# One 512-column product for the high and low halves of the sample's input, in 80 tiles of a two-layer encoder

## The reference

```
D_MODEL, SEQ, DEC_SEQ, DEPTH, D_FF = 1024, 512, 256, 2, 4096

def trunk(x, mem, p):
    for layer in range(DEPTH):
        ...                                     # mixer; its output goes through a 1024x1024 matrix
        x = x + y.astype(x.dtype)
        h = rms_norm(x, p['norm_cross'][layer])
        ...
        x = x + cross_attention(h, m, ...)       # ends in  o.astype(h.dtype) @ w_o
        h = rms_norm(x, p['norm_mlp'][layer])
        x = x + (jnp.square(jax.nn.relu(h @ p['mlp_w1'][layer])) @ p['mlp_w2'][layer]).astype(x.dtype)
    return x
```

## Time and profile before

| | value |
|---|---|
| median of three executions | 2402.44 us |
| the profiled execution's own time | 2402.41 us |
| its span, first to last instruction | 2400.6 us |
| TensorE busy | 2389.2 us (100%) |
| VectorE busy | 1512.3 us (63%) |
| ScalarE busy | 1166.6 us (49%) |
| granted TensorE clock | 1.0 throughout |
| DMA | mean 121 GB/s, weights 512 KB a tile |

### The profile page before, as it was taken

The page is one execution under the profiler, slowest core; times in us unless marked ns, Lnnn a source line. Parts: engine busy times, 40 slices in busy tenths (PEclk is TensorE's granted clock), DMA queues, the critical chain, the costliest instruction groups (busy, mean ns, idle before and its releaser), DMA issues.

```text
span 2400.6 us, 35749 instructions
## 1 busy us (share of the span) xinstructions
PE 2389.2 (100%) x14327; PEld 2050.2 (85%) x14327; DVE 1512.3 (63%) x2554; ACT 1166.6 (49%) x2070; POOL 0.2 (0%) x4
## 2 busy tenths in 40 slices
PE   9999999999999999999999999999999999999999
PEld 6988877888889998998789888888888898888887
DVE  8999668776566555664655438848985565533332
ACT  5334455555445555545454436636764453523432
POOL 0000000000000000000000000000000000000000
PEclk9999999999999999999999999999999999999999
DMA  5446533553124654443234323233234323433332
GB/s 201 106 98 164 209 110 103 165 202 123 62 88 150 192 185 132 132 133 105 76 112 149 96 88 123 89 101 100 89 100 148 122 80 117 126 98 98 97 97 89
DMA packets 109700, 291.36 MB, mean 121 GB/s; under 512 B 18944, under 2 KB 40576, under 8 KB 108256
## 3 DMA queue, kind: packets, MB, share of 16 engines
q1 hardware_dynamic: 100832, 264.83, 35.5%
q10 hardware_dynamic: 8704, 24.25, 3.3%
HBM read 267.45 MB, written 19.50 MB: 120 GB/s over the span
## 4 chain that ended last, share of the span: by engine, by line
PE 86%; DVE 3%; ACT 1%; issue 0%; DVEq 0%; ACTq 0%
PE ps L1499 74%; PE ps L1613 2%; PE ps L1570 2%; PE ps L1595 2%; PE ps L1637 1%; PE ps L1626 1%; DVE wlo L1476 1%; PE ps L1583 0%; DVE ringP L1886 0%; PE ps L1644 0%; PE ps L1991 0%; PE ps L2056 0%; PE ps L1513 0%; DVE in_lP L1893 0%; PE ps L1525 0%
## 5 line engine op out<-in xcount | busy, mean ns | idle before, releaser
L1471 ACT ACTIVATE whi<-wraw 128x1024 fp32r<-128x1024 f32 x430 | 452.1, 1052 | 183.5 <-PE ps L1499 127.1
L1499 PE MATMUL ps<-in_hP,whi 128*128 128x512 f32 x1336 | 532.8, 399 | 1.7 <-DVE in_lP L1893 0.9
L1476 DVE TENSOR_TENSOR wlo<-wraw,whi 128x1024 fp32r<-128x1024 f32 x430 | 522.9, 1218 | 3.1 <-ACT whi L1471 2.9
L1499 PE MATMUL ps<-in_hP,wlo 128*128 128x512 f32 x1336 | 520.8, 390 | 0.0
L1499 PE MATMUL ps<-in_lP,whi 128*128 128x512 f32 x1336 | 520.2, 389 | 0.0
L1499 PE MATMUL ps<-in_hS,whi 128*128 128x256 f32 x1088 | 316.0, 290 | 0.5 <-DVE x L1830 0.5
L1499 PE MATMUL ps<-in_hS,wlo 128*128 128x256 f32 x1088 | 307.7, 283 | 0.0
L1499 PE MATMUL ps<-in_lS,whi 128*128 128x256 f32 x1088 | 307.7, 283 | 0.0
L1499 PEld LDWEIGHTS ps<-in_hP,whi 128*128 128x128 f32 x1336 | 250.8, 188 | 60.5 <-issue 6.6
L1499 PEld LDWEIGHTS ps<-in_hP,wlo 128*128 128x128 f32 x1336 | 250.7, 188 | 53.5
L1499 PEld LDWEIGHTS ps<-in_lP,whi 128*128 128x128 f32 x1336 | 251.0, 188 | 51.7 <-issue 1.4
(11 more groups left out here) (494 smaller groups left out, 3662.6 us busy)
## 6 DMA issues: line engine op xcount, KB each, us to landing
wraw<-wt SPq DMA_DIRECT2D x432, 512.0 KB, 3.5
wraw<-wt ACTq DMA_DIRECT2D x17, 512.0 KB, 4.4
k_scratch<-region_P SPq DMA_DIRECT2D x16, 256.0 KB, 3.1
v_scratch<-vtmp SPq DMA_DIRECT2D x32, 128.0 KB, 3.5
x<-x_in SPq DMA_DIRECT2D x4, 768.0 KB, 7.0
x<-x_in SPq DMA_DIRECT2D x2, 1536.0 KB, 7.1
mix_mem<-mem_in ACTq DMA_DIRECT2D x1, 2048.0 KB, 15.7
region_S<-k_scratch ACTq DMA_DIRECT2D x2, 1024.0 KB, 7.1
```

The costliest lines, as they stand in the source:

```text
L1471: nc.scalar.activation(whi[:, (n + 3) % NHI, :, :], wraw[:, ws(n), :, :], ACT.Copy).then_inc(wh.sem, 1)
L1476: nc.vector.tensor_tensor(wlo[:, ws(n), :, :], wraw[:, ws(n), :, :], whi[:, (n + 3) % NHI, :, :].bitcast(F32), ALU.subtract).then_inc(wr.s ...
L1499: last = nc.tensor.matmul(ps[:, m % 2, 0:N[prod.g]], w_[:, k, :], x_[:, k, :], start=(k == 0 and j == 0), stop=(k == KT - 1 and j == 2))
```

## The change

It concerns tiles of the sample alone, those whose weights are in the list `WIDE`: the output matrix `o0` of the first cross-attention (8 tiles), up00 to up03 and dn00 to dn03 (the whole first MLP, 64 tiles) and `dout`, the output matrix of the second mixer (8 tiles). That is 48 residual tiles and 32 up tiles.

- High and low input parts now lie side by side in one SBUF tensor (`in_S`, `hid_S`; `hid_P` too, whose products are not changed), so that TensorE takes both in one product of 512 columns with the high weights. High x high lands in columns 0 to 255 of the bank, high x low in columns 256 to 511; low x high (256 columns) is accumulated on the first half. A step `k` has two products in place of three.
- Somebody must add the two halves. In residual tiles VectorE adds both to `x`, one after the other, with a semaphore between them. In up tiles VectorE first sums the halves with a `tensor_reduce` from PSUM to `ringS` (which frees the bank), ACT works on `ringS` in SBUF in place of PSUM, and the subtraction for `hid_l` (`dve_up_low`) stands one slot later on VectorE, behind the next low part of weights.

```
@@ trunk_tail
-                hid_h[g] = sb(f"hid_h{g}", [P, KT, N[g]], F32R, on=over)
-                hid_l[g] = sb(f"hid_l{g}", [P, KT, N[g]], F32R, on=over)
+                hid = sb(f"hid_{g}", [P, KT, 2, N[g]], F32R, on=over)
+                hid_h[g], hid_l[g], hid_w[g] = hid[:, :, 0, :], hid[:, :, 1, :], hid[:, :, :, :]
...
-            in_h = {"P": in_hP, "S": sb("in_hS", [P, KT, TS], F32R, on=fl)}
-            in_l = {"P": in_lP, "S": sb("in_lS", [P, KT, TS], F32R, on=fl)}
+            in_S = sb("in_S", [P, 2, KT, TS], F32R, on=fl)
+            in_h = {"P": in_hP, "S": in_S[:, 0, :, :]}
+            in_l = {"P": in_lP, "S": in_S[:, 1, :, :]}
...
+            WIDE = {WT[n] for n in ("dn00", "dn01", "dn02", "dn03", "dout", "o0", "up00", "up01", "up02", "up03", )}
...
@@ pe_tile
+                if prod.g == "S" and prod.wide is not None:
+                    for k in range(KT):
+                        if i == 0 and prod.ready is not None:
+                            pe.wait_ge(*prod.ready(k))
+                        nc.tensor.matmul(ps[:, m % 2, :].rearrange("p (z t) -> p z t", z=2), w_h[:, k, :], prod.wide[:, k, :, :],
+                                         start=(k == 0), stop=False)
+                        last = nc.tensor.matmul(ps[:, m % 2, 0:N["S"]], w_l[:, k, :], h_[:, k, :], start=False, stop=(k == KT - 1))
+                    last.then_inc(td.sem, 1)
+                    return
@@ act_tile
+                elif prod.kind == "up" and prod.wide is not None:
+                    a.wait_ge(tf[b].sem, m // 2 + 1)
+                    both = ring["S"][:, i % 2, :]
+                    act_chain(nc.scalar.activation(both, both, ACT.Relu))
+                    act_chain(nc.scalar.activation(both, both, ACT.Square))
+                    nc.scalar.activation(hid_h[g][:, i, :], both, ACT.Copy).then_inc(z["hx"].sem, 1)
@@ vector engine
+            def dve_up_low(v, t):
+                prod, i, m = t
+                v.wait_ge(gs["S"]["hx"].sem, prod.up.hx + i + 1)
+                nc.vector.tensor_tensor(hid_l["S"][:, i, :], ring["S"][:, i % 2, :], hid_h["S"][:, i, :].bitcast(F32), ALU.subtract)\
+                    .then_inc(low_d.sem, 1)
...
+                    if g == "S" and prod.wide is not None:
+                        dve_chain(nc.vector.tensor_tensor(x[:, i, cols(g)], ps[:, b, TS:2 * TS], x[:, i, cols(g)], ALU.add))
                     nc.vector.tensor_tensor(x[:, i, cols(g)], ps[:, b, 0:N[g]], x[:, i, cols(g)], ALU.add).then_inc(tf[b].sem, 1)
...
+                elif prod.kind == "up" and prod.wide is not None:
+                    v.wait_ge(td.sem, m + 1)
+                    both = ring["S"][:, i % 2, :]
+                    nc.vector.tensor_reduce(both, ps[:, b, :].rearrange("p (z t) -> p t z", z=2), AX.X, ALU.add).then_inc(tf[b].sem, 1)
...
                             lows = t[2] + NHI - 1
+                        if before is not None and before[0].kind == "up" and before[0].wide is not None:
+                            dve_up_low(v, before)
```

More of the change, by code:

```diff
@@ L975, in trunk_tail @@
             fl = ExitStack()
-            hid_h, hid_l, R = {}, {}, {}
+            hid_h, hid_l, hid_w, R = {}, {}, {}, {}
             for g, words in (("P", 12288), ("S", 6144)):
                 over = ExitStack()
-                hid_h[g] = sb(f"hid_h{g}", [P, KT, N[g]], F32R, on=over)
-                hid_l[g] = sb(f"hid_l{g}", [P, KT, N[g]], F32R, on=over)
+                hid = sb(f"hid_{g}", [P, KT, 2, N[g]], F32R, on=over)
+                hid_h[g], hid_l[g], hid_w[g] = hid[:, :, 0, :], hid[:, :, 1, :], hid[:, :, :, :]
                 over.close()
@@ L1048, in trunk_tail @@
             tf = [sig(f"tf{i}") for i in range(2)]
+            low_d = sig("low_d")
             gs = {g: {n: sig(f"{n}_{g}") for n in ("sqd", "sql", "acd", "ssum", "sroot", "snew", "an", "ah", "ar", "ap", "hx",
@@ L1098, in __init__ @@
                     self.hx = gs[g]["hx"].take(KT)
-                    self.m = {}
+                    self.m, self.low = {}, None
                 def ready(self, k):
                     m = self.m[k]
+                    if self.low is not None:
+                        return low_d.sem, self.low + k + 1
                     return tf[m % 2].sem, m // 2 + 1
@@ L1199, in __init__ @@
                     self.rhs = (in_h[g], in_l[g]) if rhs is None else rhs
+                    self.wide = None
+                    if g == "S" and kind in ("res", "up") and w0 in WIDE:
+                        if kind == "up":
+                            up.low = low_d.take(n)
+                        self.wide = hid_w[g] if rhs is not None else in_S[:, :, :, :].rearrange("p z k t -> p k z t")
                     self.norm, self.up = norm, up
```

## The result

The changed kernel takes 2407.82 us (median of 20 runs, 2403.2 to 2410.35), the kernel before 2402.46 us (20 runs in the same sessions): ratio 1.0017, 95% interval 1.0011 to 1.0024. It is 5.4 us slower, clear of the noise; 2400.2 was forecast, with 2407.5 as the upper end of the range. The profiled execution took 2408.7 us, with a span of 2406.9 us where before had 2400.6.

The account below looks back on a forecast made before the run. The prediction took TensorE's queue of products to bound the kernel: 2402.4 us, less 8.5 for shorter steps, plus waits of 1.4, 1.15, 0.85 and 2.87, gave 2400.2 us. The 8-in-10 range was 2397.0 to 2407.5.

Parts of the forecast that it names:

- The alternation of lengths I price at nothing: TensorE in wide tiles: mixing 512- and 256-column products adds no time, since weight loads stay hidden.
- forecast 8.5 us: TensorE in all wide tiles: 0.0133 us saved in each of 640 steps, 0.3467 in place of 0.3600 us.
- dout's "0 to 0.1 us": dout: a late weight load makes the low weights end at 1266.99, costing TensorE 0 to 0.1 us.
- the reduction: VectorE in up tiles: summing the halves from PSUM takes 0.69 us; the forecast built on it had chance 0.66.
- The rival of a slow stride: VectorE in up tiles: the reduction takes 1.12 us for its stride, total 2407.4 us; chance 0.16.
- The rival of 420: VectorE in up tiles: the reduction costs as its outputs, 0.42 us, paybacks 3.6 us, total 2397.5 us; chance 0.12.
- the four paybacks: First MLP: TensorE waits of 1.4 us (quiet handovers), 1.15 (statistic), 0.85 (norm's pieces) and 2.87 (up00 to dn00).
- tile 4: up00: the norm's statistic delays the reduction of tile 2, so tile 4 starts 1.15 us late.
- tiles 5 and 7: up00: the norm's pieces delay reductions on VectorE; tile 5 is 0.44 us late and tile 7 0.40, 0.85 us.
- dn00 2.87: Handover up00 to dn00: TensorE waits 2.87 us before step 7 for the last low piece.
- the quiet handovers: Up to down in up01 to up03: TensorE waits 0.47 us each before step 7, 1.4 us in three.
- The rival "no gain on TensorE": TensorE in wide tiles: a two-piece product or the length change costs the 0.0133 us saved, total 2408.7 us; chance 0.06.

Follow-up runs that it names:

- e7: e3 with the low weights' product also 512 columns wide, so all products of a wide tile are equally long: 2433.29 us, a single execution.
- e1: The changed kernel with a tile's eight 512-column products before its eight of 256, in 70 of 80 wide tiles: 2405.12 us, ratio 1.0009.
- e9: The kernel before with only the 8 tiles of dout wide, K/V load not moved: 2404.45 us, ratio 1.0008.
- e2: The changed kernel with dout as before, the other 72 tiles wide: 2404.16 us, ratio 1.0004.
- e4: The changed kernel with the K/V load of the sample's second cross-attention (2 MB) 13 slots later: 2404.19 us, ratio 1.0006.
- e11: The kernel before with only the 8 tiles of up00 wide: 2409.26 us, ratio 1.0024.
- e3: The kernel before with only dn00 to dn03 and o0 wide (40 residual tiles): 2400.69 us, ratio 0.9990.
- e5: The changed kernel without up00 (72 tiles wide), with the K/V load 13 slots later: 2399.66 us, ratio 0.9987.
- e6: The kernel before with only the 48 residual tiles wide, 512-column products first in all but a product's first tile, K/V load late: 2399.98 us, ratio 0.9985.
- e10: e5 with the product order of e1 (72 tiles wide without up00, K/V load late, grouped): 2398.41 us, ratio 0.9982.

## Why the prediction was wrong, step by step

**Wrong: "The alternation of lengths I price at nothing".** Of the forecast 8.5 us the profiled execution got about 5.5: adding back the waits below, up00 and dn00 together give 1.05 us, the six other MLP blocks 3.4, o0 0.61, dout 0.43. 3.0 us are missing. The even 0.1200 of equal lengths says nothing about mixed ones. e7 shows that without a change of length there is no loss, e1 that fewer changes lose less, and the patterns (0.3467 and 0.3533 on average) that a change has no single price. What in TensorE makes a pattern, and what picks it, stays open. The fixed 2.5 ns a product of the Trainium skill (page "TensorE: Matmul & The Clock Gate", section "Wait — 56ns, not 53.3ns?") had been set aside for rows; e7's 0.2267, 13.4 ns over 512 columns at 2.4 GHz, bears that out, and the 1.6 us of gain by that page and my 8.5 both missed the 5.5.

**Wrong: dout's "0 to 0.1 us"**, measured 2.24 us of stall. The sum compared the end of the low weights with the start of TensorE's next tile and forgot what stands behind them on VectorE, the adds that free the bank. In before, the add at 1266.90 ends at 1267.32 and TensorE restarts 0.14 later, at 1267.46, for a tile due at 1267.65: 0.2 us of margin. The change takes 0.33 from it (the tile is due earlier) and 0.46 (the second add): 0.6 us of the 2.24. The prediction could have had this term, and by its own 0.64 in place of 0.33 it would have been 0.9. The other 1.57 is the weights' own delay. The K/V load is issued 0.40 us later from the block's start (4.09 for 3.69), since it stands on ScalarE's queue behind the copy that waits for the second add. The rest of the delay is in the load itself: V lands 11.2 us after its issue and not 10.0, and the weights land 0.2 us behind it, as before. e9 and e1 have 11.1 too, e2, with dout narrow, 9.6. Why the load takes longer beside a wide dout stays open; that the collision is needed is shown by e4, where stall and delay are gone.

**Missing: a term for the clock behind a stall.** The sum had stalls, and each at its own length. In the changed kernel's dout, and in dn00 of e4 and e11, the granted clock falls to 1.2 GHz for some 3.4 us, beginning 0.5 to 1.5 us after the end of a pause of 1.9 to 2.5 us, which costs 1.5 to 1.6 us. Behind five pauses of the same size it does not: dn00 of the changed kernel, of e1 and of e2, and dout of e1 and e9. So a stall of this size costs its length or some 1.6 us more. The times of the changed kernel spread over 7.2 us, those of the four kernels without the added stalls (e3, e5, e6, e10) over 1.7 to 2.6; but e2 and e11, which stall in dn00, spread over no more (2.6 and 2.1), so the spread alone doesn't show the falls. The clock also falls near 409 us, ahead of every wide tile, in seven of the fourteen profiles, so a pause caused by the change isn't its only occasion. What decides between one run and the next stays open.

**Right: the reduction.** 0.69 us was taken, changed kernel, by line and shape:
```profile
L1878 DVE TENSOR_REDUCE ringS<-ps 128x256 f32<-128x512 f32 x32 | 22.1, 689 | 7.4 <-PE ps L1512 7.3
```
The rival of a slow stride would have shown 1120; pairs 1 KB apart cost nothing here. Its time, 2407.4, was close to the measured one by luck: none of its mechanism is there. The rival of 420 is refuted too.

**Right: the four paybacks.** Forecast and measured, start to start with the late product behind: tile 4 1.15 and 1.14; tiles 5 and 7 0.44 + 0.40 and 0.38 + 0.28; dn00 2.87 and 2.80; the quiet handovers 0.47 each and 0.39 to 0.44. PE at the second of these, changed kernel:
```profile
814.76 0.28 PE L1512 MATMUL ps<-hid_S,wlo 128*128 128x256 f32 x1
815.17 0.50 PE L1510 MATMUL ps<-hid_S,whi 128*128 128x512 f32 x1
```
(0.41 for 0.12, and 0.34 for 0.24.) Sum 6.27 forecast, 5.8 measured. The reduction ahead of the bank and the subtraction one slot later came together in every run, so what each alone would cost is argued from the timelines and not tested.

**The rival "no gain on TensorE"** ("the change of length costs the 0.0133 it saves") was half right, and at 0.06 too cheap: in the slow pattern the change of length takes half of the saving.

The account closes: from 2400.2, +3.0 for the steps, +2.24 and +1.5 for dout, +1.7 for the clock near 409 and +0.4 for the start, -0.5 for smaller paybacks is 2408.5; the profiled execution took 2408.7. Of these, the 1.7 near 409 us and the later start of 0.4 aren't the change's.

## What to carry to other kernels

Where a price is taken from a cadence of equal instructions, measure the mixed cadence before it is multiplied by 640; put equal lengths side by side. Grouping isn't the best pattern (0.3495 us a step against 0.3467), but a grouped block without a wait gained 0.54 to 0.67 us each time, an ungrouped one 0.42, 0.61 or 0.85. Take each block's edit by itself: of one edit, 8 tiles (up00) lost 5.4 us in their own stretches (6.6 by the medians), and the other 72 gained 3.1 without them and with the K/V load moved, and 4.2 grouped as well. When an edit adds work to a queue, look at every place where that queue is already late by a few tenths, with all that stands behind the late instruction, before the average room is counted.

## What the hardware showed that I had not expected

- Alternating products of 512 and 256 columns run in self-repeating patterns, of 0.3467 or 0.3533 us a pair on average, and stay in one until something interrupts them, such as a stall; the same code got either.
- The granted clock fell to its lower level for some 3.4 us behind three of eight pauses of 1.9 to 2.5 us of a TensorE that had been busy around them, and in seven of fourteen profiles near 409 us.
- A 512-column product whose columns are in two pieces that lie apart in SBUF costs 0.227 us like any other (o0 of e7).
- With K and V (1 MB each) on their way, the next 512 KB of weights landed only 0.2 us after V, 8.3 us after their own issue before the change and 10.0 after it; with this load moved away it was 3.3 (e4).
